# Fourth mixing tile of each expert pair behind the transposes of the MLP rows

## The reference

```python
def hierarchical_moe(xn, wg, bg, we, be, w_gate, w_up, w_down):
    ...
    expert = (g_idx[:, None] * EXPERTS_PER_GROUP + top_i).reshape(-1)
    order = jnp.argsort(expert)
    tok = order // TOP_K
    ...
    xs = xf[tok]
    h = jax.nn.silu(lax.ragged_dot(xs, w_gate, sizes)) * lax.ragged_dot(xs, w_up, sizes)
    y = lax.ragged_dot(h, w_down, sizes) * weights.reshape(-1)[order][:, None]
    out = jax.ops.segment_sum(y, tok, num_segments=T)
    return out.reshape(B, S, D)
```

## Time and profile before

| | |
|---|---|
| time, median of 3 runs | 2025.04 us (2019.4 to 2025.61) |
| the profiled execution | 2020.29 us, its span 2018.6 us |
| PE busy | 1900.5 us (94% of the span) |
| DVE busy | 780.0 us (39%) |
| ACT busy | 545.1 us (27%) |
| transfers | 490.10 MB, mean 243 GB/s; 415 GB/s while experts run |

### The profile page before, as it was taken

One profiled execution on the slowest core, in us unless ns is written; L12 is line 12 of the kernel. 1 busy time (PEld: TensorE's weight loads), 2 busy tenths in 40 slices (PEclk: granted clock), 3 DMA queues, 4 the chain that ended last, 5 costly groups with the idle time before them and its releaser, 6 DMA issues.

```text
span 2018.6 us, 23152 instructions
## 1 busy us (share of the span) xinstructions
PE 1900.5 (94%) x9616; PEld 1237.0 (61%) x9616; DVE 780.0 (39%) x1184; ACT 545.1 (27%) x1008; POOL 98.9 (5%) x122
## 2 busy tenths in 40 slices
PE   6999999898999999999799969989899999999997
PEld 5875777676454454454588869967675544544543
DVE  4466564535222222222433363354353222223222
ACT  3426352533111111110244332334451111111110
POOL 2200010000000000000100050000000000000000
PEclk8999999999999999999899989989999999999999
DMA  6210342125999999999424203333026999999996
GB/s 231 84 63 21 105 146 84 43 86 189 404 416 409 416 418 414 415 416 417 171 93 146 86 19 105 102 108 104 25 104 276 419 413 414 416 416 411 416 414 279
DMA packets 99931, 490.10 MB, mean 243 GB/s; under 512 B 7760, under 2 KB 16016, under 8 KB 50544
## 3 DMA queue, kind: packets, MB, share of 16 engines
q1 hardware_dynamic: 96928, 478.18, 60.1%
q0 software_dynamic: 2320, 8.29, 1.2%
q10 hardware_dynamic: 576, 2.10, 0.3%
HBM read 486.44 MB, written 2.10 MB: 242 GB/s over the span
## 4 chain that ended last, share of the span: by engine, by line
PE 87%; DVE 6%; ACT 3%; issue 2%; DMA 1%; POOL 1%; POOLq 0%; DVEq 0%; SPq 0%; ACTq 0%
PE ps L626 26%; PE ps L991 22%; PE ps L1006 11%; PE ps L956 6%; PE ps L623 6%; PE ps L977 6%; PE ps L913 1%; PE ps L800 1%; PE ps L894 1%; PE ps L970 1%; DVE wl L513 1%; DMA slot<-in_moe_w_down 1%; PE ps L645 1%; ACT wh L504 1%; DVE nat L1646 1%
## 5 line engine op out<-in xcount | busy, mean ns | idle before, releaser
L513 DVE TENSOR_TENSOR wl<-ring,wh 128x512 fp32r<-128x512 f32 x280 | 192.1, 695 | 387.7 <-ACT wh L504 386.7
L991 PE MATMUL ps<-ring,xg 128*64 128x512 f32 x1536 | 339.8, 594 | 0.3
L504 ACT ACTIVATE wh<-ring 128x512 fp32r<-128x512 f32 x280 | 174.2, 629 | 428.2 <-PE ps L626 350.5
L991 PEld LDWEIGHTS ps<-ring,xg 128*64 128x64 f32 x1536 | 107.3, 137 | 211.2 <-issue 210.5
L626 PE MATMUL ps<-wh,ah 128*128 128x512 f32 x544 | 217.7, 400 | 7.3 <-DVE wl L513 3.1
L626 PE MATMUL ps<-wl,ah 128*128 128x512 f32 x544 | 214.8, 395 | 0.0
L626 PE MATMUL ps<-wh,al 128*128 128x512 f32 x544 | 214.4, 394 | 0.0
L2108 DVE SCALAR_TENSOR_TENSOR hh<-ps,wcol,sg 128x512 f32<-128x512 f32 x32 | 36.9, 1153 | 394.8 <-PE ps L991 394.8
L2129 DVE TENSOR_TENSOR x<-ps,x 128x1024 f32<-128x1024 f32 x128 | 150.8, 1220 | 84.6 <-PE ps L977 84.6
L1006 PE MATMUL ps<-ring,hT 128*64 128x512 f32 x768 | 171.9, 595 | 10.3 <-issue 8.1
L1534 ACT ACTIVATE xg<-ps,grow 128x256 f32<-128x256 f32 x128 | 53.6, 471 | 286.9 <-PE ps L956 266.6
(11 more groups left out here) (302 smaller groups left out, 2693.3 us busy)
## 6 DMA issues: line engine op xcount, KB each, us to landing
ring<-in_moe_w_gate SPq DMA_DIRECT2D x96, 1024.0 KB, 11.1
ring<-in_moe_w_up SPq DMA_DIRECT2D x96, 1024.0 KB, 8.8
ring<-in_moe_w_down SPq DMA_DIRECT2D x96, 1024.0 KB, 8.1
slot<-in_moe_w_up SPq DMA_DIRECT2D x32, 1024.0 KB, 9.3
slot<-in_moe_w_gate SPq DMA_DIRECT2D x32, 1024.0 KB, 11.9
slot<-in_moe_w_down SPq DMA_DIRECT2D x32, 1024.0 KB, 9.7
ring<-in_x_wkv SPq DMA_DIRECT2D x16, 1024.0 KB, 5.1
ring<-in_c_w_in SPq DMA_DIRECT2D x16, 1024.0 KB, 5.3
```

The costliest lines, as they stand in the source:

```text
L504: act.activation(wh[:, t % STAGE, :], ring[:, unit % RING, 512 * s:512 * (s + 1)], ACT.Copy).then_inc(wh_ready, 1)
L513: dve.tensor_tensor(wl[:, t % STAGE, :], ring[:, unit % RING, 512 * s:512 * (s + 1)], wh[:, t % STAGE, :].bitcast(F32), ALU.subtract).then ...
L991: mm = pe.matmul(ps[p * SLOTS:(p + 1) * SLOTS, bank, :], xg[:, b % 2, k, r * P + p * SLOTS:r * P + (p + 1) * SLOTS], w(p)[:, k % 4, :], st ...
```

## The change

In `pair`, `do_mix(q - 1, 3, MIX)` moves from directly behind `do_mix(q - 1, 2, Y)` to directly behind `hidden_T`. No instruction is added or removed, and no semaphore or count is changed. DVE, ACT, POOL and SP keep their lists.

```diff
@@ -1120,10 +1120,11 @@
                         do_gather(b + 1, 2 * (q % 2), GATHER)
                     if q:
                         do_mix(q - 1, 2, Y)
-                        do_mix(q - 1, 3, MIX)
                     pe.wait_ge(S["h_ready"], q0 + q + 1)
                     after(pe, S["hT_ready"], q0 + q)
                     hidden_T().then_inc(S["hT_done"], 1)
+                    if q:
+                        do_mix(q - 1, 3, MIX)
                     if q + 1 < PAIRS:
                         do_weights(q + 1)
                         do_slots(q + 1)
```

## The result

| | before | with the change |
|---|---|---|
| median | 2025.04 us (2019.4 to 2025.61) | 2032.09 us (2029.84 to 2032.93) |
| the profiled execution, its span | 2020.29 us, 2018.6 us | 2029.84 us, 2028.0 us |
| ratio | | 1.0047, 95% interval 1.0035 to 1.0059 |

The change makes the kernel slower by 0.47%, some 9.5 us; the medians lie 7.1 us apart. The forecast was 8.0 us more, and 2033.0 us.

What follows compares the result with a forecast made beforehand. The prediction took PE to bound the kernel, with tile 3's addition releasing the down products; 5.7 us (26 pairs) plus 2.3 us (four late pairs) made 8.0 us, 2025.04 + 8.0 = 2033.0 us, range 2023.0 to 2035.5 us.

Steps and rivals of the forecast that it cites:

- the releaser: Ahead of the down products: the addition of tile 3 releases them in all 30 pairs, load 0.06 to 0.08 behind it.
- The transposes and the copy: Transposes of `hh` start earlier and copy `hT` ends some 0.9 us earlier, but nothing waits for it; worth 0.
- The fourth tile: Pairs 1 to 13 of each layer: tile 3's products follow the transposes, its addition ends 0.22 us later; 5.7 us.
- the 0.08 in it: Extra distance from tile 3's first to second product, 0.31 against 0.23 us, taken as a weight load that nothing covers.
- the low rival: At the switch from transposes to tile 3, the weight load is covered: 5.6 us more, 2030.6 us; chance 0.12.
- Its sign, 0.23 or 0.31: Tile 3's second product 0.23 us behind its first would mean a covered weight load, 0.31 an uncovered one.
- Pairs 14 and 15: Without a gather `hh` comes late, PE waits, and tile 3's addition starts 0.57 us later; four such pairs, 2.3 us.
- The sum: Whole kernel: 5.7 + 2.3 = 8.0 us more, 2033.0 us against the median, 0.40% more.
- The copy as releaser: Ahead of the down products: ACT's copy `hT` releases them, 11.8 us less, 2013.2 us; chance 0.05.
- DVE's cover: Tile 2's addition hides up to 0.23 us of tile 3's delay; if enough, about 2 us more, 2027 us; chance 0.06.
- The transfers: While experts run, transfers set the pace and absorb PE's delay: no loss, 2025 us; chance 0.05.
- The clock: Longer idle time ahead of the down products, about 0.5 us, lowers PE's clock in some pairs: over 2036 us; chance 0.02.

Runs made afterwards that it cites:

- one added transpose: The kernel before, with one transpose of the identity into bank 2 put between tiles 2 and 3; ratio 1.0003 to before.
- four transposes: The kernel before, with four transposes of the identity into bank 2 put between tiles 2 and 3; ratio 1.0032 to before.
- the change with the relaxed wait: The changed kernel, its down products waiting for three additions of the pair before instead of four; ratio 0.9962 to the kernel before.
- eight transposes: The kernel before, with eight transposes of the identity into bank 2 put between tiles 2 and 3; ratio 1.0114 to before.
- pairs 1 to 13 alone: The kernel before, with the change made only in pairs 1 to 13 of each layer, 14 and 15 in the old order; ratio 1.0037 to before.

## Why the prediction was right

**The direction and the releaser.** The forecast rested on reading the load's start against two ends, 0.07 behind the addition and 0.48 behind the copy, against the profile's own attribution. Eight traces now agree with that reading. In all of them the load stands 0.07 behind the addition, in each of the 30 pairs that have one; behind the copy it stands, by the medians, anywhere from 0.26 to 2.47 us. In the two runs that no longer wait for this addition the load starts before its end.

**The transposes and the copy, worth 0.** The copy ends 1.63 us early (forecast about 1.6) and nothing comes of it.

**The fourth tile in 26 pairs, 0.22 each.** The additions are 0.23 farther apart. The stretch from the transposes to the end of the products, the term that rows of another stage had to stand for, came as there: 715.90 - 715.59 = 0.31 us from the first to the second product, and 716.37 - 715.23 = 1.14 us from the first transpose to the fourth product, forecast 1.13.

**What the 0.08 in it is.** Here the prediction was right in the number and wrong in the reason. It took the 0.31, against 0.23 in a stream, for a weight load that nothing covers. The run with one added transpose tests that. Its PE, from the third and fourth product of tile 2 on:

```profile
714.93 0.39 PE L977 MATMUL ps<-yh,selT 128*128 128x512 f32 x1
715.16 0.39 PE L977 MATMUL ps<-yl,selT 128*128 128x512 f32 x1
715.39 0.27 PE L1125 MATMUL ps<-ident 128*128 128x128 f32 x1
715.42 0.47 PE L977 MATMUL ps<-yh,selT 128*128 128x512 f32 x1
715.73 0.39 PE L977 MATMUL ps<-yl,selT 128*128 128x512 f32 x1
715.96 0.40 PE L977 MATMUL ps<-yh,selT 128*128 128x512 f32 x1
716.20 0.39 PE L977 MATMUL ps<-yl,selT 128*128 128x512 f32 x1
```

Again the second product is listed 0.31 behind the first. But from the last product of tile 2 to the last of tile 3 it takes 716.20 - 715.16 = 1.04 us, against 715.55 - 714.64 = 0.91 before: one transpose puts the tile off by 0.13. Its own step of 0.11 ((0.60 - 0.27) / 3, from the rows of four transposes and of one) and an uncovered load of 0.08 would be 0.19. With four it is 716.37 - 715.00 = 1.37, so 0.46, where four steps alone are 0.43. What is left for the switch is 0.02 to 0.03. The first product is listed 0.03 behind the last transpose (715.42 and 715.39), before that one's step of 0.11 is over, and so the distance to the second looks 0.08 too long. The 1.13 was read from transpose to fourth product, and the early listing cancels in it: four steps of 0.11 and three of 0.235 are 1.14. It didn't cancel in the price of the low rival: the 0.14 us a pair (5.6 us) takes 0.08 off a sum in which no load stands. Its sign, 0.23 or 0.31, couldn't tell a covered load from an uncovered one either; the load is as good as covered, and the additions are 0.23 farther apart all the same.

**What was short.** A pair lost 0.27, not 0.22. That term was 0.04 to 0.05 short, 1 us over the 26 pairs: 0.02 of it stands ahead of the down products, and 0.02 behind them, in the second gather and in tiles 0 and 1, where PE's starts lie a little farther apart (from the gather's first start to the gate products' first, 729.09 - 725.15 = 3.94 with the change, 728.46 - 724.54 = 3.92 before). That part wasn't in the sum, and no run shows what makes it; it comes with one added transpose too (median 3.94) and not with four (3.92).

**Pairs 14 and 15, 0.57 each.** Additions 0.56 farther apart, loads 0.59 and 0.55 later: as forecast.

**The sum.** 8.0 forecast; between the first and the last down products of the two layers the traces differ by 9.1 us (913.0 against 904.0 us, with rounding). The ratio gives 9.5 us (7.1 to 11.9), the medians 7.1. That the median of 2032.09 us lies in the range of 2023.0 to 2035.5 says little by itself, since the time of before lies in it as well; the ratio and the rows carry the account.

**The rivals.** The copy as releaser fell twice over: the load moved when only the wait for additions was relaxed, and stayed when the copy was made later. DVE's cover exists, but at 0.23 us it is half of the 0.46 that the change asks of it, and the run with one transpose shows the case in which it suffices. The transfers absorb nothing: a usual pair grows by all that the addition is late. The clock stays at 1.00 with 0.5 us of idle time ahead of the down products, so nothing is lost to it.

**A version that beats both.** The order of before with the down products waiting for three additions takes 0.9958 of the time of before (2012.43 us, median of 5). The wait was for one addition more than the banks need, and what the change set out to move was not on the path.

## What to carry to other kernels

Where an instruction waits for two semaphores, measure its start against the end of each candidate in several pairs, and take the one whose distance stays the same; the profile's attribution can name the other one every time. Before work is moved ahead of something, ask what it pushes back, and whether that is what the next stage waits for. A wait with a count is worth checking against the banks it protects: here one less was enough, and paid more than any order of the products tried here.

## What the hardware showed

- The listed start of the first 512-column product behind 128-column transposes is 0.08 us early, so the second is listed 0.31 us behind it instead of 0.23, with one transpose ahead as with four; the tile as a whole loses 0.11 us per transpose and 0.02 to 0.03 for the switch. The Trainium skill (TensorE: Matmul & The Clock Gate, the step-by-step part on LDWEIGHTS) has weight loads pulled ahead of running matmuls. The changed kernel agrees: the load for this first product starts at 715.56, together with the last transpose (715.34 + 0.49 - 0.27 = 715.56), and delays what follows by 0.03 at most.

```profile
715.34 0.49 PE L998 MATMUL ps<-ident,hh 128*128 128x128 f32 x3
...
715.56 0.19 PEld L977 LDWEIGHTS ps<-yh,selT 128*128 128x128 f32 x1
```

- An addition of 1.22 us starts 1.14 us behind its neighbour on DVE if its input is ready, 0.08 before the neighbour's listed end. That overlap made the cover 0.23 and not 0.31 us.
- 418 GB/s of transfers beside a PE that never waits for them in 440 us: the 415 GB/s of before looked full and weren't. Single waits of 0.4 to 0.8 us for a transfer do show in the last pair of a layer in four of the ten traces (before, the change with the relaxed wait, eight transposes, pairs 1 to 13 alone).
